# The fullest expert's remainder moved into its own wide job: 192 slots in one pass over the weights

## The chip, the cores and the metric

One core of one Trainium2 chip. The time is device microseconds for one execution of the whole kernel; lower is better.

## The reference, cut to what matters

Two decoder layers run on a prompt group (256 tokens) and a sample group (64 tokens), 320 tokens in all. Layer 0 has a dense channel mixer. Layer 1 has a mixture of eight experts, of which each token takes two. Only that mixture is touched:

```python
D_MODEL, N_EXPERTS, TOP_K, D_FF_EXPERT = 1024, 8, 2, 2816

def _moe(h, w_router, b_router, w_gate, w_up, w_down):
    logits = h @ w_router + b_router
    top_vals, top_idx = lax.top_k(logits, TOP_K)
    wts = jax.nn.softmax(top_vals, axis=-1)
    combine = sum(one_hot(top_idx, N_EXPERTS) * wts[..., None], axis=-2)
    out = 0
    for e in range(N_EXPERTS):
        out += combine[..., e:e + 1] * ((silu(h @ w_gate[e]) * (h @ w_up[e])) @ w_down[e])
    return out
```

All data are float32. One expert's three matrices are 3 x 1024 x 2816 x 4 bytes, 34.6 MB. The 640 assignments of the reference's inputs (the default seed) fall on experts 0 to 7 as 54, 170, 119, 49, 73, 62, 63 and 50.

## The kernel before, in words

Everything ahead of the experts (both mixers, the dense mixer, the router) is the same in both kernels and ends at about 1208 us of the span. After it the kernel runs **jobs**. A job takes one expert's weights from HBM once and puts a block of that expert's tokens through them.

- A **narrow** job has 64 slots. Its products are plain float32. The 64 gathered rows, transposed, are the stationary operand (XEF); the raw weights in MRAW move. The gate product goes to the lower 64 columns of the array and the up product to the upper 64, so one PSUM bank holds both. The profile shows each such float32 product as two passes.
- A **wide** job has 128 slots. Its products are float32r, in three passes: ScalarE rounds the weights to MHI (line 1775), VectorE writes the remainder to MLO over MRAW (line 1163), and TensorE multiplies high tokens by high weights (2637), low tokens by high weights (2638) and high tokens by low weights (2643).

Each job has 35 **pairs**, the unit of every semaphore count: 24 for gate and up (three groups of columns, widths 512, 512 and 384 per tile, eight contraction steps each) and 11 for down. A pair is 1 MB of weights (0.75 MB in the third group) in one slot of MRAW, which has 7 slots (`RAW_RING`). The SP queue issues two DMAs for a pair as soon as `m_used` says that TensorE has finished with the slot's last tenant, so loads run at most 7 pairs ahead.

Between pairs, TensorE does **side units**, each in PSUM bank 4 or 5: in pairs 2 to 9 it places the last job's result among all tokens ("combine", two products of 320 columns), in six pairs it transposes the product of gate and up ("turn"), and it builds the placement of this job's rows ("place") and the list of the next job's rows ("pick"). GpSimd gathers those rows by an indirect DMA (line 1991), and pairs 28 and 30 transpose them ("fill"). At the end of a job ScalarE scales the result to YEH (1816 wide, 1843 narrow) and VectorE writes its remainder YEL (1403 wide, 1420 narrow) and raises `y_made`; the next job can write the result's banks only then.

The order is written out: narrow 0, wide 1, then narrow and wide in a loop up to wide 5, then narrow 6, and a loop of further narrow jobs whose number comes from the router. Expert 0 takes job 0; the others are ranked by their number of tokens, the first three take jobs 1, 3 and 5, the rest jobs 2, 4, 6 and the first of the loop. An expert with more tokens than its job's slots gets extra narrow jobs of 64, which load its weights again. With the counts above, expert 1 (170 tokens, 128 slots) gets one: nine jobs, 0 to 8.

GpSimd's queue of gathers has a fixed length, `NE + EXTRA + 1`: those that no job asked for are let go together behind the last job by `V.tensor_copy(SPARE...).then_inc(idx_made, EXTRA)` (line 1448), and run one behind another.

Of the kernel before, what the change touches and what calls it, by code (L numbers as in the profile page):

```python
# [50 lines left out]
EXTRA = 7  # L51
# [10 lines left out]
def side_units():  # L62


    units = {p: [] for p in range(PAIRS)}
    for d in range(KD):
        units[d + 2].append(("combine", d))
    for t, p in enumerate((10, 11, 18, 19, 26, 27)):
        units[p].append(("turn", t))
    units[13].append(("place", 0))  # L70
    units[16].append(("pick", 0))
    plan, number = {}, 0
# [6 lines left out]
SIDE, JAUX = side_units()  # L79
assert JAUX % 2 == 0  # L80
FILLS = {28: 0, 30: 1}
HM_TILES = (2, 0, 1)
# [4 lines left out]
FILL_BANKS = (6, 7)  # L87
GT_BANKS = ((2, 3), (5, 1))
# [11 lines left out]
TURNED = {tile_at(k)[0]: s for units in SIDE.values() for s, what, k in units if what == "turn"}  # L100
TURN_SLOT = {k: s for units in SIDE.values() for s, what, k in units if what == "turn"}
# [138 lines left out]
def build(nc, a, out):  # L240
    ctx = ExitStack()
    with ctx:
# [152 lines left out]
        IOTAH = at("iotah", [P, P], F32, o + 13536)  # L395
# [37 lines left out]
        m_tile, xe_in, xe_out, y_hi = sem("m_tile"), sem("xe_in"), sem("xe_out"), sem("y_hi")  # L433
        xe_hi, idx_made, xg_in, hd_stored = sem("xe_hi"), sem("idx_made"), sem("xg_in"), sem("hd_stored")
# [36 lines left out]
        def _(sp):  # L471
# [49 lines left out]
            def load_job(job, e, first=False):  # L521
# [3 lines left out]
                for n in range(PAIRS):  # L525
                    if not (first and n < RAW_RING):
                        sp.wait_ge(m_used, job * PAIRS + (n - RAW_RING + 1))
                    for j in range(2):
                        if n < GPAIRS:
# [18 lines left out]
            with sp.Fori(1, MAIN) as job:  # L548
                e = sp.value_load(XI[0:1, bass.ds(job, 1)], min_val=0, max_val=NE - 1)
                load_job(job, e)  # L550
# [14 lines left out]
        def _(dve):  # L565
# [606 lines left out]

            def picked(src):
# [35 lines left out]
            V.tensor_copy(IOTAH[:, HALF:P], CF[:, C_IOTA:C_IOTA + HALF])  # L1209
            st(V.tensor_tensor(XG[:, 0:P], ident, CF[:, C_IOTA:C_IOTA + P], ALU.mult))  # L1210
# [46 lines left out]
            def ranks():  # L1257
# [9 lines left out]
                st(V.tensor_scalar(KEY[:, 3, :], KEY[:, 3, :], float(MAIN), 0.0, ALU.min, ALU.max))  # L1267
                st(V.memset(KEY[:, 2, 0:1], 1.0))
# [79 lines left out]
            def side_dve(job, p, split):  # L1348

                for s, what, k in SIDE[p]:  # L1350
                    bank = 4 + s % 2
                    if what == "combine":
                        dve.wait_ge(m_aux_in, job * JAUX + (s + 1))
                        V.tensor_tensor(SA[:, k, :], SA[:, k, :], PS[:, bank, 0:T], ALU.add).then_inc(m_aux_out, 1)  # L1354
                    elif what == "turn" and split is None:
                        f0, nf = tile_at(k)
                        dve.wait_ge(gate_out, job * TURNS + (k + 1))
                        V.tensor_tensor(GTF[:, f0:f0 + nf, :],  # L1358
                                        SGT[:, k % 2, 0:nf * HALF].rearrange("p (k n) -> p k n", k=nf),
                                        PS[:, bank, 0:nf * P].rearrange("p (k n) -> p k n", k=nf)[:, :, HALF:P],  # L1360
                                        ALU.mult).then_inc(m_aux_out, 1)
                    elif what == "turn":
                        f0, nf = tile_at(k)
                        dve.wait_ge(gt_hi, split * TURNS + (k + 1))
                        V.tensor_tensor(GTL[:, f0:f0 + nf, :],
                                        PS[:, bank, 0:nf * P].rearrange("p (k n) -> p k n", k=nf),
                                        GTH[:, f0:f0 + nf, :].bitcast(F32), ALU.subtract).then_inc(m_aux_out, 1)
                    elif what == "place":
                        dve.wait_ge(m_aux_in, job * JAUX + (s + 1))
                        V.tensor_copy(PTS[:, :], PS[:, bank, 0:T]).then_inc(m_aux_out, 1)  # L1370
                    else:
                        dve.wait_ge(m_aux_in, job * JAUX + (s + 1))
                        V.tensor_copy(IW[:, :], PS[:, bank, 0:2]).then_inc(m_aux_out, 1)
                        dve.wait_ge(m_aux_out, job * JAUX + (AHEAD + s + 1))
                        V.tensor_copy(IDX[:, :], IW[:, 1:2]).then_inc(idx_made, 1)
# [8 lines left out]
            def wide_dve(job, split):  # L1384
# [3 lines left out]
                for p in range(PAIRS):  # L1388
# [22 lines left out]
                    side_dve(job, p, split)  # L1411
# [3 lines left out]
            def narrow_dve(job, split_next=None, first=False):  # L1415

                for p in range(PAIRS):
# [8 lines left out]
                    side_dve(job, p, None)  # L1426
                    if p == 14:
                        choose(job + 1, split_next is None)
                    if first and p in TABLE_PAIRS:
                        tables(TABLE_PAIRS[p])  # L1430
                if split_next is not None:
                    for n in range(2):
                        m_lo_part(split_next, n)

            narrow_dve(0, 0, first=True)
            wide_dve(1, 0)
            with dve.Fori(1, WIDE) as two:
                narrow_dve(two * 2, two)
                wide_dve(two * 2 + 1, two)
            narrow_dve(2 * WIDE)  # L1440
            dve.wait_ge(sem("routed"), 1)
            extra = dve.value_load(XI[0:1, 15:16], min_val=1, max_val=1 + EXTRA)
            with dve.Fori(0, 1 + EXTRA) as k:
                with dve.If(k < extra):
                    narrow_dve(k + MAIN)
# [24 lines left out]
        def _(act):  # L1470
# [306 lines left out]
            def gathered(k, number, half):  # L1777

                act.wait_ge(xe_in, number + 1)
                src = PS[:, FILL_BANKS[k], :].rearrange("p (k n) -> p k n", k=4)  # L1780
# [18 lines left out]
            for k in range(2):  # L1799
                gathered(k, k, True)  # L1800

            def wide_act(job):
# [3 lines left out]
                for p in range(PAIRS):  # L1806
# [13 lines left out]
                    for s, what, k in SIDE[p]:  # L1820
                        if what == "turn":
                            f0, nf = tile_at(k)
                            act.wait_ge(m_aux_in, job * JAUX + (s + 1))
                            A.activation(GTH[:, f0:f0 + nf, :],
                                         PS[:, 4 + s % 2, 0:nf * P].rearrange("p (k n) -> p k n", k=nf), ACT.Copy)\
                                .then_inc(gt_hi, 1)
# [3 lines left out]
            def narrow_act(job, half_next):  # L1830
                A.activation(SPARE[:, 0:1], ONES[:, 0:1], ACT.Silu)
                for p in range(PAIRS):
# [11 lines left out]
                    for s, what, k in SIDE[p]:  # L1844
                        if what == "turn":
                            nf = tile_at(k)[1]
                            act.wait_ge(m_aux_in, job * JAUX + (s + 1))
                            if k >= 2:
                                act.wait_ge(m_aux_out, job * JAUX + (AHEAD + TURN_SLOT[k - 2] + 1))
                            A.activation(SGT[:, k % 2, 0:nf * HALF].rearrange("p (k n) -> p k n", k=nf),  # L1850
# [919 lines left out]
```

## Time and profile before

| | |
|---|---|
| time, median of three runs | 2053.22 us (2049.69 to 2054.38) |
| the profiled execution's own time | 2054.07 us |
| its span in the trace | 2052.2 us |
| TensorE busy | 1911.1 us, 93% of the span |
| VectorE, ScalarE busy | 969.0 us, 743.1 us |
| mean granted TensorE clock | 0.978 |
| read from HBM | 510.87 MB |

The busy share of TensorE is high in every stage, whether it works or not: ends of matrix products are modelled, and a run of passes counts as one busy stretch. What limits a stage is seen better from its DMA rate and from the distance between the starts of like instructions. The nine jobs take the stretch from 1208 to 2016 us. In a windows view the columns behind the stretch and its length are the busy time (and number) of TensorE's products, TensorE's weight loads, VectorE, ScalarE and GpSimd, then the granted clock as a share of full speed, the DMA share and GB/s.

### The profile page before, as it was taken

The numbers are of one execution on the slowest core, as the hardware profiler recorded it, in microseconds if no ns is written. First come the engines' busy times: TensorE is split into PE (matmuls) and PEld (weight loads), VectorE is DVE, ScalarE is ACT, GpSimd is POOL, SyncE is SP. The second block draws the span as 40 slices with busy tenths as digits, with TensorE's granted clock in tenths as the row PEclk, the third lists the DMA queues.
The fourth block names the chain that finished last, engine by engine and source line by source line (L and its number), as shares of the span: only waits on it lengthen the run. The fifth ranks groups of instructions, "written<-read, shape, count | busy, mean of one in ns | idle before, by whom it ended". The sixth has DMA issues, their size and how long they took to land. (4 is left out here: it accounts for less than half of the span.)

```text
span 2052.2 us, 31765 instructions
## 1 busy us (share of the span) xinstructions
PE 1911.1 (93%) x12573; PEld 1481.2 (72%) x12573; DVE 969.0 (47%) x1350; ACT 743.1 (36%) x928; POOL 132.3 (6%) x173
## 2 busy tenths in 40 slices
PE   7999999999999989999999999999899989989884
PEld 4999999997999979999999853684387358523221
DVE  4476554555444355765455432881385168401011
ACT  4434333434434353433344321661364156210011
POOL 3100002200000030000041100000000000000001
PEclk9999999999999999999999989999999999999997
DMA  9635355573666545334656369999989998999994
GB/s 353 208 99 170 116 182 181 177 250 99 210 204 213 172 131 184 103 108 154 185 190 212 139 231 407 358 355 406 409 307 394 408 391 325 408 407 407 409 408 170
DMA packets 243670, 525.43 MB, mean 256 GB/s; under 512 B 18103, under 2 KB 142121, under 8 KB 243538
## 3 DMA queue, kind: packets, MB, share of 16 engines
q1 hardware_dynamic: 233440, 492.63, 66.8%
q0 software_dynamic: 10080, 30.86, 4.7%
q8 instruction: 100, 1.64, 0.3%
q14 instruction: 32, 0.26, 0.0%
q10 hardware_dynamic: 18, 0.04, 0.0%
HBM read 510.87 MB, written 12.59 MB: 255 GB/s over the span
## 5 line engine op out<-in xcount | busy, mean ns | idle before, releaser
L577 DVE TENSOR_TENSOR wlo<-raw,whi 128x1024 fp32r<-128x1024 f32 x244 | 289.1, 1212 | 313.7 <-ACT whi L1484 312.4
L2094 PE MATMUL ps<-h1h,whi 128*128 128x320 f32 x1248 | 387.1, 322 | 6.8 <-DVE h1l L684 3.9
L2095 PE MATMUL ps<-h1l,whi 128*128 128x320 f32 x1248 | 372.3, 310 | 0.0
L1484 ACT ACTIVATE whi<-raw 128x1024 fp32r<-128x1024 f32 x244 | 247.7, 1046 | 118.6 <-PE ps L2479 44.8
L2683 PE MATMUL ps<-mraw,xef 128*64 128x512 f32 (+1 forms) x1152 | 251.9, 567 | 22.1 <-DMA mraw<-in_w_exp_up 16.7
L2094 PEld LDWEIGHTS ps<-h1h,whi 128*128 128x128 f32 x1248 | 236.6, 190 | 23.2 <-issue 17.5
L2095 PEld LDWEIGHTS ps<-h1l,whi 128*128 128x128 f32 x1248 | 236.7, 190 | 0.2 <-issue 0.2
L1163 DVE TENSOR_TENSOR mlo<-mraw,mhi 128x2048 fp32r<-128x2048 f32 (+1 forms) x105 | 225.4, 2165 | 16.4 <-ACT mhi L1775 16.4
L1775 ACT ACTIVATE mhi<-mraw 128x2048 fp32r<-128x2048 f32 (+1 forms) x105 | 190.6, 1819 | 84.8 <-DMA mraw<-in_w_exp_up 32.6
L2140 PE MATMUL ps<-h1h,wlo 128*128 128x320 f32 x1248 | 209.7, 310 | 0.0
L2140 PEld LDWEIGHTS ps<-h1h,wlo 128*128 128x128 f32 x1248 | 189.6, 188 | 0.4 <-issue 0.4
L2683 PEld LDWEIGHTS ps<-mraw,xef 128*64 128x64 f32 x1152 | 72.5, 136 | 146.2 <-issue 99.1
L2701 PE MATMUL ps<-mraw,gtf 128*64 128x512 f32 x528 | 127.8, 605 | 30.7 <-DMA mraw<-in_w_exp_down 28.7
L2637 PE MATMUL ps<-mhi,xeh 128*128 128x512 f32 (+1 forms) x288 | 115.3, 400 | 8.0 <-ACT mhi L1775 8.0
L2701 PEld LDWEIGHTS ps<-mraw,gtf 128*64 128x64 f32 x528 | 32.1, 136 | 109.7 <-DMA mraw<-in_w_exp_down 65.8
L2638 PE MATMUL ps<-mhi,xel 128*128 128x512 f32 (+1 forms) x288 | 110.4, 383 | 0.0
L1354 DVE TENSOR_TENSOR sa<-sa,ps 128x320 f32<-128x320 f32 x72 | 35.0, 486 | 119.5 <-PE ps L2554 119.5
L1358 DVE TENSOR_TENSOR gtf<-sgt,ps 128x256 f32<-128x256 f32 (+1 forms) x36 | 14.4, 399 | 160.4 <-ACT sgt L1850 160.4
L1840 ACT ACTIVATE sg<-ps 128x512 f32<-128x512 f32 (+1 forms) x36 | 20.2, 562 | 183.0 <-PE ps L2683 183.0
L2643 PE MATMUL ps<-mlo,xeh 128*128 128x512 f32 (+1 forms) x288 | 78.4, 384 | 1.6 <-DVE mlo L1163 1.6
L2094 PE MATMUL ps<-h2h,whi 128*128 128x320 f32 x256 | 77.0, 315 | 0.0
L2095 PE MATMUL ps<-h2l,whi 128*128 128x320 f32 x256 | 75.5, 309 | 0.0
(446 smaller groups left out, 2763.4 us busy)
## 6 DMA issues: line engine op xcount, KB each, us to landing
mraw<-in_w_exp_down SPq DMA_DIRECT2D x198, 512.0 KB, 12.7
mraw<-in_w_exp_gate SPq DMA_DIRECT2D x144, 512.0 KB, 7.4
mraw<-in_w_exp_up SPq DMA_DIRECT2D x144, 512.0 KB, 9.1
raw<-in_w_in SPq DMA_DIRECT2D x128, 512.0 KB, 3.9
raw<-in_w_ada SPq DMA_DIRECT2D x64, 512.0 KB, 3.8
mraw<-in_w_exp_gate SPq DMA_DIRECT2D x72, 384.0 KB, 7.2
mraw<-in_w_exp_up SPq DMA_DIRECT2D x72, 384.0 KB, 9.2
pause<-in_w_ada SPq DMA_DIRECT2D x32, 512.0 KB, 7.0
```

The lines of the kernel that those rows point to most:

```text
L577: V.tensor_tensor(WLO[:, u % RAW_UNITS, 0:w], RAW[:, u % RAW_UNITS, 0:w], WHI[:, h % HI_UNITS, 0:w].bitcast(F32), ALU.subtract).then_inc(l ...
L1163: V.tensor_tensor(MLO[:, n % RAW_RING, 0:w], MRAW[:, n % RAW_RING, 0:w], MHI[:, n % HI_RING, 0:w].bitcast(F32), ALU.subtract).then_inc(m_l ...
L1484: A.activation(WHI[:, h % HI_UNITS, 0:w], RAW[:, u % RAW_UNITS, 0:w], ACT.Copy).then_inc(hi_made, 1)
L1775: A.activation(MHI[:, n % HI_RING, 0:w], MRAW[:, n % RAW_RING, 0:w], ACT.Copy).then_inc(m_hi, 1)
L2094: M.matmul(out_, w, v[0], start=start, stop=False, skip_group_check=True)
L2095: M.matmul(out_, w, v[1], start=False, stop=False, skip_group_check=True)
L2140: ins = M.matmul(PS[:, 2 * j + m, 0:T], w[1][:, s], parts[0][:, k * T:(k + 1) * T], start=False, stop=(k == KD - 1), skip_group_check=True)
L2637: M.matmul(o_, XEH[:, k, :], hi_[:, s], start=(k == 0), stop=False)
L2638: M.matmul(o_, XEL[:, k, :], hi_[:, s], start=False, stop=False)
L2643: ins = M.matmul(PS[:, GROUP_BANKS[g][2 * i + j], 0:w], XEH[:, k, :], lo_[:, s], start=False, stop=(k == KD - 1))
L2683: ins = M.matmul(PS[HALF * j:HALF * j + HALF, GROUP_BANKS[g][2 * i], 0:w], XEF[:, k, :], MRAW[:, p % RAW_RING, s], start=(k == 0), stop=(k ...
L2701: ins = M.matmul(PS[HALF * h:HALF * h + HALF, DOWN_BANKS[0], :], GTF[:, kf, :], MRAW[:, p % RAW_RING, s], start=(kf == 0), stop=(kf == KF ...
```

## The change

The fullest of experts 1 to 7 keeps job 1, which now has 192 slots and is called **both**. The first 128 are done in three passes as before; slots 128 to 191 are done in plain float32 from the same raw weights in MRAW. The table of extra jobs gives this expert one block fewer, and `EXTRA` goes from 7 to 6. Jobs 3 and 5 stay wide.

- MRAW must now stay raw, so the remainder goes to two of the five MHI slots: three slots for the high part (`BOTH_HI`), two for the remainder (`BOTH_LO`).
- A pair of gate and up in job 1 is two contraction steps of one tile instead of one step of two tiles; the loads have the same number and bytes, with runs of 512 (384) columns instead of 1024 (768).
- The order on TensorE within a pair: raw pass, high passes, remainder pass.
- Job 0 has no combine (nothing precedes it), but a second pick (pair 12), gather (XG2) and fill (pairs 20 and 21) for slots 128 to 191. Job 1 has six more turns and one more place. Job 2's combine has four products instead of two.
- ScalarE and VectorE make a third result part (YEH2, YEL2) at the end of job 1, and job 1's first product waits for job 0's `y_made`.
- Jobs 2 and 3 are written out; the loop runs once, for jobs 4 and 5.

```diff
-EXTRA = 7
+EXTRA = 6
+BOTH_BANKS = ((3, 7, 2), (0, 1, 6))
+BOTH_HI, BOTH_LO = 3, 2
...
+                        if both and n < GPAIRS:
+                            (c0, w), k = cols_at(n // 4), 2 * (n % 4)
+                            sp.dma_start(MRAW[:, n % RAW_RING, 2 * w * j:2 * w * (j + 1)].rearrange("p (k n) -> p k n", k=2),
+                                         (g, u)[j][:, k:k + 2, c0:c0 + w]).then_inc(m_raw[n % RAW_RING], 16)
...
+            def both_lo_part(job, n):
+                w = 4 * GROUPS[n // KD][1] if n < GPAIRS else 2 * D
+                dve.wait_ge(m_hi, n + 1)
+                if n >= BOTH_LO:
+                    dve.wait_ge(m_used, job * PAIRS + (n - BOTH_LO + 1))
+                V.tensor_tensor(MHI[:, BOTH_HI + n % BOTH_LO, 0:w], MRAW[:, n % RAW_RING, 0:w],
+                                MHI[:, n % BOTH_HI, 0:w].bitcast(F32), ALU.subtract).then_inc(m_lo, 1)
...
+                st(V.tensor_scalar(KEY[:, 5, :], KEY[:, 1, :], 1.5, None, ALU.is_lt))
+                st(V.tensor_tensor(KEY[:, 2, :], KEY[:, 2, :], KEY[:, 5, :], ALU.subtract))
...
+            def both_hi_part(job, n):
+                if n >= BOTH_HI:
+                    act.wait_ge(m_used, job * PAIRS + (n - BOTH_HI + 1))
...
+                        A.activation(SG2[:, 0:w], PS[:, BOTH_BANKS[t % 2][2], 0:w], ACT.Copy).then_inc(copied2, 1)
...
-            for job in range(NE + EXTRA + 1):
+                if job == 1:
+                    pool.wait_ge(idx_made, 2)
+                    pool.indirect_dma_start(XG2[:, :], None, HD, bass.IndirectOffsetOnAxis(IDX2[:, 0:1], 0)).then_inc(xg_in, 16)
+                    pool.wait_ge(xg_in, 32)
...
+                def gate_up_both(p):
+                    t, (_, w) = p // 4, cols_at(p // 4)
+                    gate_, up_, both_ = BOTH_BANKS[t % 2]
+                    raw_, hi_, lo_ = raw_in(p)
+                    if p == 0:
+                        pe.wait_ge(y_made, job + 1)
+                    for n in range(2):
+                        k = 2 * (p % 4) + n
+                        for j in range(2):
+                            M.matmul(PS[HALF * j:HALF * j + HALF, both_, 0:w], XEF2[:, k, :],
+                                     raw_[:, (2 * j + n) * w:(2 * j + n + 1) * w], start=(k == 0), stop=(k == KD - 1),
+                                     skip_group_check=True)
+                    pe.wait_ge(m_hi, p + 1)
+                    for n in range(2):
+                        k = 2 * (p % 4) + n
+                        for j, bank in enumerate((gate_, up_)):
+                            s = slice((2 * j + n) * w, (2 * j + n + 1) * w)
+                            M.matmul(PS[:, bank, 0:w], XEH[:, k, :], hi_[:, s], start=(k == 0), stop=False)
+                            M.matmul(PS[:, bank, 0:w], XEL[:, k, :], hi_[:, s], start=False, stop=False)
+                    pe.wait_ge(m_lo, p + 1)
...
-            narrow_pe(0, False)
-            wide_pe(1, 0, True)
-            with pe.Fori(1, WIDE) as two:
-                narrow_pe(two * 2, False)
-                wide_pe(two * 2 + 1, two, True)
+            narrow_pe(0, SIDE_FIRST, None)
+            both_pe(1)
+            narrow_pe(2, SIDE, "both")
+            wide_pe(3, 1, "narrow")
+            with pe.Fori(2, WIDE) as two:
```

## Rows read from the trace of the kernel before

**Rows 1.** The page, DMA issues: times issued, KB each, us to landing.
```profile
mraw<-in_w_exp_down SPq DMA_DIRECT2D x198, 512.0 KB, 12.7
```

**Rows 2.** Stretches of one expert job each: busy of each engine, clock, DMA, GB/s.
```profile
1286.00:1393.00 107.00, 104.51 (x479) 85.23 (x481) 85.97 (x64) 69.50 (x52) 0.94 (x1) 0.97 0.95 359
1393.00:1471.00 78.00, 70.98 (x333) 23.71 (x329) 10.71 (x26) 7.72 (x18) 0.95 (x1) 1.00 1.03 407
...
1844.00:1930.00 86.00, 73.33 (x339) 23.56 (x335) 8.65 (x24) 7.30 (x17) 0.95 (x1) 1.00 1.03 408
1930.00:2016.00 86.00, 72.81 (x335) 23.37 (x331) 8.69 (x24) 7.03 (x15) 0.95 (x1) 1.00 0.97 386
```

**Rows 3.** TensorE's timeline at the ends of jobs 0, 1 and 2: start, us, idle before.
```profile
1283.65 1.03 PE L2701 MATMUL ps<-mraw,gtf 128*64 128x512 f32 x4
1287.41 0.47 PE L2637 MATMUL ps<-mhi,xeh 128*128 128x512 f32 x1 [2.74 <-ACT mhi L1775]
...
1289.65 1.22 PE L2643 MATMUL ps<-mlo,xeh 128*128 128x512 f32 x2 [1.07 <-DVE mlo L1163]
...
1392.23 1.94 PE L2683 MATMUL ps<-mraw,xef 128*64 128x512 f32 x8
...
1468.70 1.94 PE L2701 MATMUL ps<-mraw,gtf 128*64 128x512 f32 x8 [0.62 <-DMA mraw<-in_w_exp_down]
```

**Rows 4.** VectorE's timeline: the last operation of jobs 0, 1, 7 and 8.
```profile
1285.51 0.75 DVE L1420 SCALAR_TENSOR_TENSOR yel<-ps,sw,yeh 128x512 fp32r<-128x512 f32 x1 [9.12 <-ACT yeh L1843]
...
1393.06 1.41 DVE L1403 SCALAR_TENSOR_TENSOR yel<-ps,sw,yeh 128x512 fp32r<-128x512 f32 x2 [6.39 <-ACT yeh L1816]
...
1929.72 0.75 DVE L1420 SCALAR_TENSOR_TENSOR yel<-ps,sw,yeh 128x512 fp32r<-128x512 f32 x1 [17.52 <-ACT yeh L1843]
...
2015.71 0.75 DVE L1420 SCALAR_TENSOR_TENSOR yel<-ps,sw,yeh 128x512 fp32r<-128x512 f32 x1 [17.44 <-ACT yeh L1843]
```

**Rows 5.** ScalarE's timeline at the end of wide job 1.
```profile
1392.34 1.27 ACT L1816 ACTIVATE yeh<-ps,sw 128x512 fp32r<-128x512 f32 x2 [7.86 <-PE ps L2668]
```

**Rows 6.** TensorE's timeline in narrow job 2 (xcount: passes in the run).
```profile
1394.52 3.65 PE L2683 MATMUL ps<-mraw,xef 128*64 128x512 f32 x16 [0.36 <-DVE yel L1403]
1398.11 0.42 PE L2553 MATMUL ps<-pts,yeh 128*128 128x320 f32 x1
...
1398.60 1.94 PE L2683 MATMUL ps<-mraw,xef 128*64 128x512 f32 x8
1400.46 0.41 PE L2553 MATMUL ps<-pts,yeh 128*128 128x320 f32 x1
...
1433.03 1.51 PE L2683 MATMUL ps<-mraw,xef 128*64 128x384 f32 x8
```

**Rows 7.** TensorE's timeline in wide job 1: two turns; a pair's start, the next side unit.
```profile
1327.31 0.60 PE L2586 MATMUL ps<-cf,sg 128*128 128x128 f32 x4
...
1330.50 0.60 PE L2586 MATMUL ps<-cf,sg 128*128 128x128 f32 x4
...
1333.70 0.39 PE L2637 MATMUL ps<-mhi,xeh 128*128 128x512 f32 x1
...
1336.43 0.49 PE L2589 MATMUL ps<-cf,pm 128*128 128x128 f32 x3
```

**Rows 8.** Two stretches at the start of wide job 1 (columns as in Rows 2).
```profile
1285.00:1290.00 5.00, 1.51 (x5) 1.03 (x6) 3.26 (x3) 4.18 (x3) 0.00 (x0) 0.86 1.03 411
1290.00:1296.00 6.00, 6.00 (x16) 4.62 (x16) 5.16 (x3) 4.00 (x3) 0.00 (x0) 0.55 1.02 405
```

**Rows 9.** Groups of instructions by line: busy, mean ns, idle before.
```profile
L1163 DVE TENSOR_TENSOR mlo<-mraw,mhi 128x2048 fp32r<-128x2048 f32 x81 | 183.9, 2287 | 12.9 <-ACT mhi L1775 12.9
...
L1775 ACT ACTIVATE mhi<-mraw 128x2048 fp32r<-128x2048 f32 x81 | 155.0, 1917 | 60.2 <-DMA mraw<-in_w_exp_up 24.7 <-DMA mraw<-in_w_exp_down 24.1 <-PE ps L2643 10.7
```

**Rows 10.** GpSimd's timeline after the last job.
```profile
2020.29 0.95 POOL L1991 DMA_INDIRECT xg<-h_rows,idx  x1 [46.72 <-DVE spare L1448]
...
2044.91 0.95 POOL L1991 DMA_INDIRECT xg<-h_rows,idx  x1 [3.29 <-DMA xg<-h_rows,idx]
```

More of the change, by code:

```diff
@@ L59, with side_units @@
 AHEAD = 2
-def side_units():
+def side_units(turns, others, start=0):
     units = {p: [] for p in range(PAIRS)}
-    for d in range(KD):
-        units[d + 2].append(("combine", d))
-    for t, p in enumerate((10, 11, 18, 19, 26, 27)):
+    for p, what, k in others:
+        units[p].append((what, k))
+    for t, p in enumerate(turns):
         units[p].append(("turn", t))
-    units[13].append(("place", 0))
-    units[16].append(("pick", 0))
-    plan, number = {}, 0
+    plan, number = {}, start
     for p in range(PAIRS):
@@ L1346, in table_out @@
                 see.next(sem("routed"))
[L1348 to L1375, printed above, removed]
@@ L1410, in wide_dve @@
                         next_weight(job)
-                    side_dve(job, p, split)
+                    for s, what, k in SIDE[p]:
+                        if what == "combine":
+                            combine_dve(job * JAUX, s, k)
+                        elif what == "turn":
+                            low_turn(s, k, gt_hi, split * TURNS + (k + 1))
+                        elif what == "place":
+                            place_dve(PTS, job * JAUX, s)
+                        else:
+                            pick_dve(IW, IDX, idx_made, job * JAUX, s)
@@ L1417, in narrow_dve @@
+            def narrow_dve(job, side, split_next=None):
                 for p in range(PAIRS):
@@ L1425, in narrow_dve @@
                         low_fill(FILLS[p - 1], split_next)
-                    side_dve(job, p, None)
+                    for s, what, k in side[p]:
+                        if what == "combine":
+                            combine_dve(job * JAUX, s, k)
+                        elif what == "turn":
+                            half_turn(GTF, s, k, gate_out, job * TURNS + (k + 1))
+                        elif what == "place":
+                            place_dve(PTS, job * JAUX, s)
+                        elif what == "pick2":
+                            pick_dve(IW2, IDX2, idx_made, job * JAUX, s)
+                        else:
+                            pick_dve(IW, IDX, idx_made, job * JAUX, s)
+                    if side is SIDE_FIRST and p in TABLE_PAIRS:
+                        tables(TABLE_PAIRS[p])
+                    if side is SIDE_FIRST and p == 9:
+                        choose2(job + 1)
                     if p == 14:
                         choose(job + 1, split_next is None)
[L1429 to L1436, printed above, removed]
+            narrow_dve(0, SIDE_FIRST, 0)
+            for n in range(BOTH_LO):
+                both_lo_part(1, n)
+            both_dve(1)
             with dve.Fori(1, WIDE) as two:
-                narrow_dve(two * 2, two)
+                narrow_dve(two * 2, SIDE, two)
+                for n in range(2):
+                    m_lo_part(two, n)
                 wide_dve(two * 2 + 1, two)
-            narrow_dve(2 * WIDE)
+            narrow_dve(2 * WIDE, SIDE)
             dve.wait_ge(sem("routed"), 1)
@@ L2573, in _, with turn, place, side_pe @@
             pe.wait_ge(sem("gt_out"), 4)
-            def side_pe(job, p, half_before):
-                for s, what, k in SIDE[p]:
+            def turn(bank, src, nf):
+                for m in range(nf):
+                    ins = M.transpose(PS[:, bank, m * P:(m + 1) * P], src[:, m * P:(m + 1) * P], ident)
+                return ins
+            def place(bank, marks):
+                for t in range(TT):
+                    ins = M.transpose(PS[:, bank, t * P:(t + 1) * P], marks[:, t, :].bitcast(F32), ident)
+                return ins
+            def side_pe(job, p, before, side=SIDE):
+                for s, what, k in side[p]:
                     bank = 4 + s % 2
@@ L2581, in side_pe @@
                         pe.wait_ge(y_made, job + 1)
-                        ins = combine(k, bank, half_before)
+                        ins = combine_both(k, bank) if before == "both" else combine(k, bank, before == "narrow")
                     elif what == "turn":
                         pe.wait_ge(prod_made, job * TURNS + (k + 1))
-                        for m in range(tile_at(k)[1]):
-                            ins = M.transpose(PS[:, bank, m * P:(m + 1) * P], SG[:, k % 2, m * P:(m + 1) * P], ident)
+                        ins = turn(bank, SG[:, k % 2, :], tile_at(k)[1])
@@ L2587, in side_pe @@
                     elif what == "place":
-                        for t in range(TT):
-                            ins = M.transpose(PS[:, bank, t * P:(t + 1) * P], PM[:, t, :].bitcast(F32), ident)
-                    else:
-                        pe.wait_ge(p_made, job + 2)
+                        ins = place(bank, PM)
+                    elif what == "pick2":
+                        pe.wait_ge(p_made, 2)
+                        ins = pick(PS[:, bank, 0:2], PM2)
+                    else:
+                        pe.wait_ge(p_made, job + 3)
+                        ins = pick(PS[:, bank, 0:2])
@@ L2675, in narrow_pe @@
+            def narrow_pe(job, side, before):
                 pe.wait_ge(xe_out, job * 2 + 2)
@@ L2697, in narrow_pe @@
                                 pe.wait_ge(prod_made, job * TURNS + 4)
-                            turned_in(job, kf)
+                            turned_in(job * JAUX, kf, slots_of(side, "turn"))
                             for h in range(2):
```

320 lines of the change are left out of this document (266 added, 54 removed).

## The prediction, written before the result was known

> **What bounds the kernel now.** I read the DMA issues first: 198 loads of down matrices at 22 a job are nine jobs for eight experts [rows 1]. The reference's counts say whose the ninth is: expert 1 has 170 tokens and 128 slots, and no other expert exceeds its block (119 and 73 in 128; 63, 62, 54, 50, 49 in 64).
>
> Then the windows, job by job [rows 2]. Narrow jobs 7 and 8 take 86 us each, with DMA share near 1 and 386 to 408 GB/s: they are bound by the loads, 86.0 / 35 = 2.457 us a pair. The reader should not take TensorE's 73 us there for a limit. Wide job 1 takes 107 us at 359 GB/s, DMA below full: it is bound by TensorE. Narrow job 2 takes only 78 us because some pairs were loaded during job 1. The last look is at the tail: after job 8 GpSimd runs six gathers nobody asked for, the first issued at 2020.29 and the last at 2044.91, 4.9 us apart on average [rows 10], and nothing issues behind them.
>
> **What is removed.** Job 8 as a whole: from job 7's last operation to job 8's, 2015.71 - 1929.72 = **86.0 us** [rows 4]. All of it is on the path, since its loads are what the core waits for; its 70 DMAs on the SP queue, ScalarE's and VectorE's work and one gather go with it and were hidden beneath them.
>
> **What is added to job 1.** Its own work today: TensorE ends job 0 at 1283.65 + 1.03 = 1284.68, begins job 1 at 1287.41 and begins job 2 at 1392.23 [rows 3]. That is 104.8 us. In it are 1.1 us of waiting for the first remainder [rows 3] and about 2.9 us lost to the lower clock (6 us at a granted 0.55 lose 2.7, the second half of the stretch before about 0.2 [rows 8]). At full clock and without waits job 1 is 100.8 us of TensorE.
>
> 1. Raw passes. A narrow pair of width 512 is eight passes. A run of 16 takes 3.65 us and one of 8 takes 1.94 [rows 6], so a pair costs 1.71 and the rest is the last pass's tail. Width 384: 1.51 - 0.23 = 1.28. So 27 x 1.71 + 8 x 1.28 = **56.4 us**.
> 2. Changes of array shape. Raw products run as 128*64, the others as 128*128, so a pair has two changes more. The trace has no raw pass beside a high pass; the nearest row is the combine in a narrow job. From one combine to the next 2.35 us pass (1398.11 to 1400.46) [rows 6], 1.71 of them raw, so 0.64 is left for two products of 320 columns and two changes. A wide pair of 12 products of 512 columns takes 2.73 us (1333.70 to 1336.43) [rows 7], 0.2275 each; two of 320 columns are 0.28 by that, and 0.36 are the changes. I take 0.36 x 35 = **12.6 us**. The bounds are 0 (a change that hides behind the stream) and 0.64 (all of it): 0 to 22.4.
> 3. Six more turns: a pair with a turn takes 3.19 (1327.31 to 1330.50), without 2.73 [rows 7]: 0.46 x 6 = **2.8 us**. One more place is three transposes, at most a turn: **0.3**.
> 4. The start. The new job's first product waits for job 0's `y_made`, raised at 1285.51 + 0.75 = 1286.26 [rows 4]; it needn't wait for ScalarE's copy, so it starts at 1286.3 instead of 1287.4. While the raw pass runs (1.7) ScalarE makes the first high part (1.92) and VectorE the remainder (2.29) behind it [rows 9], done near 1290, about when TensorE has done raw and high passes.
>
> The sum is 1286.3 + 100.8 + 56.4 + 12.6 + 2.8 + 0.3 = 1459.2, against 1392.23: **+67.0 us**.
>
> Of TensorE's clock: after 2.74 us of idle and a few scattered products it was granted 0.86, then 0.55 [rows 3, 8], so partly the lower level, 1.2 GHz. The idle is now 1.6 us and the work behind it dense, so I charge nothing and keep 4 us for the upper end.
>
> **What stays hidden in job 1.** A pair takes 1.71 + 2.73 + 0.36 = 4.8 us on TensorE. VectorE's remainder for pair n may start when TensorE begins pair n-1, and is wanted 1.71 + 0.2 + 1.8 = 3.7 us into pair n: 8.5 us for 2.29 of work. Ahead of it in VectorE's order is at most the wait for ScalarE's silu at a tile's end, the product of gate and up, and a turn, whose high part stands behind another 1.92 us copy: together near 4 us. ScalarE's high part has two pairs' time. A load has seven pairs of 4.8 us for 2.46 us of transfer, so the shorter runs (2 KB and 1.5 KB) cost nothing; only pair 0 could land later, beneath the wait for `y_made`. SP issues as many DMAs as before. The second pick, gather and fill go into job 0, which waits for loads anyway (TensorE 1.71 of 2.46 us a pair), and it loses eight combines. The two new table operations and the second selection on VectorE are there too. GpSimd's extra gather stands ahead of job 2's, eight pairs earlier.
>
> **Job 2.** Its start finds the ring full instead of partly full, but `y_made` comes later. Now ScalarE takes 1.27 us for two parts [rows 5], and VectorE ends at 1393.06 + 1.41 = 1394.47 [rows 4], 2.24 after TensorE. With a third part on each, 3.5. The first slots come free when two more pairs' halves are done, at 3.5 + 1.8 = 5.3 us. From there 28 pairs must be loaded: 68.8 us, plus some 2 to 4 us until a transfer lands in an empty queue, plus 1.94: 78 to 80. Before it was 1468.70 + 1.94 - 1392.23 = 78.4 [rows 3]. So **0**, within 2 us. The four-product combine makes TensorE's pair about 2.8 instead of 2.35; the two slots freed at once cover most of eight times 0.3.
>
> **The tail.** Released gathers before: fixed length 16, less ten used. After: 15 plus the separate one, less ten used (first, second selection, eight jobs). Six again, so the last job's end to the span's end stays 36 us.
>
> Sum: -86.0 + 67.0 + 0 = **-19.0 us**. On the profiled execution, 2054.07, that is 2035.1; it lay 0.85 above the median of 2053.22, so **2034 us**.
>
> On item 2 the Trainium skill has a rule against this change: TensorEngine Tiling (Array Packing), under Key Properties, says that changing the tiling mode, as opposed to the tile, drains TensorE; and TensorE: Matmul & The Clock Gate, under Single matmul latency, puts the drain near 175 ns. An estimate from these pages is 70 changes x 0.175 = 12.3 us, with which the time would be 0.3 us lower. The trace agrees with a cost at each change (0.36 for two), and no run here shows yet that high passes behind raw ones pay the same.
>
> **The rivals.**
> - *Forecast* (0.70): job 1 dense on TensorE, as summed. Alone it spans 2024 to 2045.
> - *Dear changes and a lower clock* (0.12): 0.64 a pair instead of 0.36 gives +9.8, the clock +4: 2048. For it: each change comes with a semaphore wait. Against: wide jobs wait twice a pair without a gap.
> - *Late copies in the smaller ring* (0.06): only three high and two remainder slots. If both copies ran after the preceding pair had ended, the remainder would be ready 1.92 + 2.29 = 4.2 us into the pair instead of 3.7 wanted: 0.5 x 35 = +18, 2052, no change. Against: the waits permit an earlier start.
> - *The two halves of the array don't overlap* (0.04), the slower side. If a raw pass between two changes of shape ran its gate and up products one after the other, it would take twice as long: +56.4, 2090. It decides from a third of the passes on (19 / 56.4). Against: raw runs between two combines are also eight passes long and show the full rate [rows 6].
> - *Nine jobs stay* (0.01): then 86.0 is not taken off: 2120. Against: 170 is at most 192.
> - *More is given back* (0.07): changes almost free and job 2 gains 2 us: 2023 to 2026.
>
> The range is 2022 to 2048: it leaves out the slower cases and half of the dear one, near 0.17. Faster by over 0.2% (4 us, about what a measurement of this kernel can tell from no change) is forecast, dear and giving back: 0.89. Same 0.06, slower 0.05.
>
> **What the profile after would show.** 176 loads of down matrices. Job 1 from `y_made` to the next raw run near 173 us, with clock near 1.00 and DMA near 200 GB/s (34.6 MB in 173 us). Pairs of width 512 without side units start 4.8 us apart: 5.1 means dear changes, 6.5 halves in turn. TensorE's waits for the high part or remainder in job 1 near zero. Job 2 near 78 us, job 7 (now the last) 86, six gathers and 36 us behind it. The prediction is wrong if the pair's spacing is off by over 0.4 us, or if TensorE waits at each tile's end.

## The result, and the profile after

The changed kernel takes **2034.55 us** (median of five runs, 2029.12 to 2037.92) against 2053.22 (2049.69 to 2058.04): a ratio of 0.9901, 95% interval 0.9878 to 0.9925. The forecast was 2034, range 2022 to 2048.

The page's DMA issues show eight jobs, 176 / 22 [rows 1], and 476.26 MB read from HBM instead of 510.87:

```profile
HBM read 476.26 MB, written 12.59 MB: 241 GB/s over the span
...
mraw<-in_w_exp_down SPq DMA_DIRECT2D x176, 512.0 KB, 12.0
```

The windows after, job 1 (both), job 2, and the last job, 7 (columns as in [rows 2]):

```profile
1283.00:1456.00 173.00, 172.40 (x784) 102.67 (x786) 90.29 (x71) 73.87 (x63) 0.94 (x1) 1.00 0.68 230
1456.00:1537.00 81.00, 74.64 (x351) 26.36 (x347) 11.37 (x27) 8.25 (x19) 0.95 (x1) 1.00 0.98 378
...
1906.00:1992.00 86.00, 73.29 (x335) 23.67 (x335) 8.76 (x23) 7.35 (x17) 0.94 (x1) 1.00 0.98 388
```

Job 1 is where the work went: TensorE full, clock 1.00, and DMA only 0.68 busy, where the two stretches it replaces had DMA near full [rows 2]. Its 230 GB/s are more than the 200 that the forecast gave as a sign: 39.8 MB in 173 us instead of 34.6. In the first 17 us of the job DMA still runs at about 386 GB/s, so the ring was not yet full when job 1 began. VectorE's timeline gives the last operation of jobs 0, 1, 2 and 7, as in [rows 4]:

```profile
1282.71 0.75 DVE L1524 SCALAR_TENSOR_TENSOR yel<-ps,sw,yeh 128x512 fp32r<-128x512 f32 x1 [9.16 <-ACT yeh L2007]
...
1456.83 1.41 DVE L1495 SCALAR_TENSOR_TENSOR yel<-ps,sw,yeh 128x512 fp32r<-128x512 f32 x2 [8.64 <-ACT yeh L1981]
1458.15 0.74 DVE L1497 SCALAR_TENSOR_TENSOR yel<-ps,iw,yeh 128x512 fp32r<-128x512 f32 x1
...
1537.69 0.75 DVE L1524 SCALAR_TENSOR_TENSOR yel<-ps,sw,yeh 128x512 fp32r<-128x512 f32 x1 [9.12 <-ACT yeh L2007]
...
1992.59 0.75 DVE L1524 SCALAR_TENSOR_TENSOR yel<-ps,sw,yeh 128x512 fp32r<-128x512 f32 x1 [17.42 <-ACT yeh L2007]
```

With the same operations of every job the difference of the two profiled spans, 2028.9 - 2052.2 = -23.3 us, divides without a remainder. Lengths in us, from one job's last operation to the next one's:

| | to end of job 0 | 1 | 2 | 3 | 4 | 5 | 6 | 7 | 8 | behind the last job |
|---|---|---|---|---|---|---|---|---|---|---|
| before | 1285.51 | 107.55 | 78.41 | 106.76 | 80.87 | 106.81 | 77.78 | 86.03 | 85.99 | 36.49 |
| after | 1282.71 | 174.12 | 80.86 | 106.28 | 78.10 | 106.28 | 78.37 | 85.87 | none | 36.31 |
| difference | -2.80 | +66.57 | +2.45 | -0.48 | -2.77 | -0.53 | +0.59 | -0.16 | -85.99 | -0.18 |

Jobs 1, 2 and 8 are where the forecast put the change. Their sum is -17.0, and the medians moved by 18.7. The first column is the scatter of single executions: in the traces of the changed kernel and its variants below, job 0 ends anywhere from 1281.11 to 1291.33. That scatter is why the lengths of jobs are compared below, and whole times only where they differ by more.

Job 4's -2.77 is another matter. Job 4 takes 80.87 and 79.82 us in the two traces of the old loop (before, and experiment 10) and 77.5 to 79.3 in all ten of the new one. Before, TensorE stood idle ahead of job 4's first product, and no releaser is shown for it; in the changed kernel the first eight passes start at once:

```profile
1579.66 5.37 PE L2683 MATMUL ps<-mraw,xef 128*64 128x512 f32 x24 [2.18 <-issue]
```

```profile
1643.14 1.94 PE L2980 MATMUL ps<-mraw,xef 128*64 128x512 f32 x8
1645.43 3.65 PE L2980 MATMUL ps<-mraw,xef 128*64 128x512 f32 x16 [0.35 <-DVE yel L1464]
```

Experiment 10, with the old loop, has 2.30 us of idle there, and none of the ten others has more than 0.36. It is the place where the old loop over two jobs begins its second round; the new one has a single round, since jobs 2 and 3 are written out. So some 2 us of the gain probably come from writing them out. No run isolates this.

TensorE's timeline of job 1's first pairs, after:

```profile
1279.94 1.94 PE L2998 MATMUL ps<-mraw,gtf 128*64 128x512 f32 x8 [0.67 <-DMA mraw<-in_w_exp_down]
1283.60 1.94 PE L2918 MATMUL ps<-mraw,xef 128*64 128x512 f32 x8 [1.72 <-DVE yel L1524]
1285.47 0.50 PE L2926 MATMUL ps<-mhi,xeh 128*128 128x512 f32 x1
...
1287.42 1.07 PE L2933 MATMUL ps<-mhi,xeh 128*128 128x512 f32 x4
1288.41 1.94 PE L2918 MATMUL ps<-mraw,xef 128*64 128x512 f32 x8
...
1293.27 1.94 PE L2918 MATMUL ps<-mraw,xef 128*64 128x512 f32 x8
```

The reader sees the 1.72 us for `y_made` at the start, the raw run of eight passes at its old length of 1.94, so both halves of the array still work together, and no bracket of idle time in any line behind it. Pairs of 512 columns without a side unit are 4.81 to 4.86 us apart. In the whole job the view of waits lists none of TensorE's products waiting for a copy (weight loads do, by 0.8 us at most, beneath the products); what it lists first, behind GpSimd's wait for the next list of rows, are the copies waiting for TensorE:

```profile
ACT mhi L1900 <- PE ps L2933: 42.3, 16, 3.5
DVE mhi L1223 <- PE ps L2933: 32.1, 17, 2.6
```

### The profile page after: what moved, and what is told of

It is laid out like the page before. It is cut to its first block and busy times, and to the rows that moved or that the text cites. A ratio compares the mean times of both kernels' runs of the same rounds, so it can differ in the third digit from the quotient of the medians.

```text
span 2028.9 us, 31221 instructions
## 1 busy us (share of the span) xinstructions
PE 1902.8 (94%) x12557; PEld 1474.9 (73%) x12557; DVE 962.2 (47%) x1336; ACT 741.4 (37%) x927; POOL 131.8 (6%) x173
## 3 DMA queue, kind: packets, MB, share of 16 engines
HBM read 476.26 MB, written 12.59 MB: 241 GB/s over the span
## 5 line engine op out<-in xcount | busy, mean ns | idle before, releaser
L2980 PE MATMUL ps<-mraw,xef 128*64 128x512 f32 (+1 forms) x960 | 208.2, 566 | 15.6 <-DMA mraw<-in_w_exp_up 11.9
L1199 DVE TENSOR_TENSOR mlo<-mraw,mhi 128x2048 fp32r<-128x2048 f32 (+1 forms) x70 | 150.2, 2165 | 10.1 <-ACT mhi L1892 10.0
L2980 PEld LDWEIGHTS ps<-mraw,xef 128*64 128x64 f32 x960 | 62.3, 136 | 118.3 <-issue 84.1
L2998 PE MATMUL ps<-mraw,gtf 128*64 128x512 f32 x440 | 106.6, 605 | 25.1 <-DMA mraw<-in_w_exp_down 23.6
L1223 DVE TENSOR_TENSOR mhi<-mraw,mhi 128x2048 fp32r<-128x2048 f32 (+1 forms) x35 | 75.9, 2168 | 56.8 <-PE ps L2933 32.1
L2998 PEld LDWEIGHTS ps<-mraw,gtf 128*64 128x64 f32 x440 | 26.7, 136 | 91.0 <-DMA mraw<-in_w_exp_down 58.1
L2862 PE MATMUL ps<-mhi,xeh 128*128 128x512 f32 (+1 forms) x192 | 75.5, 393 | 5.5 <-ACT mhi L1892 5.5
L2863 PE MATMUL ps<-mhi,xel 128*128 128x512 f32 (+1 forms) x192 | 72.6, 378 | 0.0
L2004 ACT ACTIVATE sg<-ps 128x512 f32<-128x512 f32 (+1 forms) x30 | 16.8, 562 | 143.3 <-PE ps L2980 143.3
```

Of the source, the lines that this page charges most:

```text
L1199: V.tensor_tensor(MLO[:, n % RAW_RING, 0:w], MRAW[:, n % RAW_RING, 0:w], MHI[:, n % HI_RING, 0:w].bitcast(F32), ALU.subtract).then_inc(m_l ...
L1223: V.tensor_tensor(MHI[:, BOTH_HI + n % BOTH_LO, 0:w], MRAW[:, n % RAW_RING, 0:w], MHI[:, n % BOTH_HI, 0:w].bitcast(F32), ALU.subtract).the ...
L2862: M.matmul(o_, XEH[:, k, :], hi_[:, s], start=(k == 0), stop=False)
L2863: M.matmul(o_, XEL[:, k, :], hi_[:, s], start=False, stop=False)
L2980: ins = M.matmul(PS[HALF * j:HALF * j + HALF, GROUP_BANKS[g][2 * i], 0:w], XEF[:, k, :], MRAW[:, p % RAW_RING, s], start=(k == 0), stop=(k ...
L2998: ins = M.matmul(PS[HALF * h:HALF * h + HALF, DOWN_BANKS[0], :], GTF[:, kf, :], MRAW[:, p % RAW_RING, s], start=(kf == 0), stop=(kf == KF ...
```

## The experiments

Each of the first eight is one edit of the changed kernel, 9 is three of them together, and 10 is an edit of the kernel before. Experiments 1, 2, 5, 6 and 7 were executed once each (1968.93, 2058.16, 2037.35, 2029.26 and 2038.62 us), so they are read by the lengths in their traces alone. In the traces of experiments 2, 3, 4, 5 and 8 and of the changed kernel, where job 2 is the same, it takes 80.8 to 81.5 us from one job's last operation to the next: differences of a few tenths say nothing.

**1. Job 1 without the raw passes.** The products into the third bank are left out in all 35 pairs, so the outputs lack slots 128 to 191.

```diff
-                            M.matmul(PS[HALF * j:HALF * j + HALF, both_, 0:w], XEF2[:, k, :], raw_[...], ...)
...
-                            ins = M.matmul(PS[HALF * h:HALF * h + HALF, BOTH_BANKS[0][2], :], GTF2[:, kf, :], raw_[...], ...)
```

> Job 1 without its raw passes (slots 128 to 191 are not computed; 42 tokens lack one expert's part). It measures terms 1 and 2 of the sum together. My theory (raw stream 56.4 us plus 70 changes of array shape): TensorE's job 1, 171.8 us in the changed kernel, falls by 68 to 70 us to 102 to 104, and TensorE waits for nothing new in it. Rival, the smaller ring of copies: with pairs now 2.73 us apart instead of 4.86 the three high and two remainder slots become the limit, TensorE waits for the high part or the remainder in many pairs, and the job falls by less, to 110 or more.

```profile
1286.88 0.47 PE L2920 MATMUL ps<-mhi,xeh 128*128 128x512 f32 x1 [2.80 <-ACT mhi L1900]
...
1391.92 1.94 PE L2970 MATMUL ps<-mraw,xef 128*64 128x512 f32 x8
```

TensorE's job 1 runs from 1286.88 to 1391.92, 105.0 us, against 171.8 (1283.60 to 1455.42). Without raw passes the start must wait for ScalarE's copy again, 2.80 us, and the clock falls again:

```profile
1285.00:1290.00 5.00, 3.12 (x9) 2.52 (x10) 3.46 (x3) 3.65 (x2) 0.00 (x0) 0.76 1.05 387
1290.00:1296.00 6.00, 6.00 (x26) 4.93 (x25) 5.23 (x4) 4.17 (x4) 0.00 (x0) 0.92 1.06 388
```

The granted 0.76 and 0.92 take 5 x 0.24 + 6 x 0.08 = 1.7 us, so at full clock the job has 103.3, and the raw passes with their changes of shape cost 68.5. The forecast's two terms were 56.4 + 12.6 = 69.0. As measured the job fell by 66.8, less than the 68 to 70 expected: the expectation did not have the lower clock. Behind the start no product waits for a copy in the job, so the smaller ring is no limit even at 2.73 us a pair.

**2. One slot for each copy.**

```diff
-BOTH_HI, BOTH_LO = 3, 2
+BOTH_HI, BOTH_LO = 1, 1
```

> One high slot and one remainder slot instead of three and two, so that both copies of a pair can only begin when TensorE has ended the pair before. Theory: the remainder is then ready 1.92 + 2.29 = 4.2 us or a little more into the pair and wanted at about 3.75, so TensorE waits some 0.5 us in each ordinary pair and about 1.5 us more in the six pairs behind a tile's end, where silu and the third copy stand ahead on ScalarE: job 1 gets 18 to 30 us longer (190 to 202). Rival, copies that hide anyway: less than 5 us longer. Rival, copies already at the limit in the changed kernel: much more than 30 us, since then the slack I count isn't there.

```profile
1303.11 0.50 PE L2926 MATMUL ps<-mhi,xeh 128*128 128x512 f32 x1 [0.19 <-ACT mhi L1900]
...
1305.43 1.20 PE L2933 MATMUL ps<-mhi,xeh 128*128 128x512 f32 x4 [0.21 <-DVE mhi L1223]
```

Both kinds of wait, absent in the changed kernel, are there, 28 times and 9.6 us in all; the rest of the longer job is not listed as a wait of TensorE's products. Job 1's length is 193.56 instead of 174.12: +19.4, at the low end of what was expected. So the ring matters, and rings of three and two are enough. The rival of late copies fell because the slots removed its cause, not because the copies are fast.

**3. The table as before.** The fullest expert gets its extra job although job 1 does all its slots, so 42 tokens count expert 1 twice.

```diff
-                st(V.tensor_tensor(KEY[:, 2, :], KEY[:, 2, :], KEY[:, 5, :], ALU.subtract))
```

> Only the table is as before: the fullest expert is given its extra job again, although job 1 does all its 192 slots (the result of 42 tokens counts expert 1 twice). It measures the removed term. Theory: one more load-bound job of 86.0 us behind the others and five gathers instead of six behind it: 2034.5 + 86 - 0 to 4 = 2116 to 2121, some 3.1 to 3.3% above the kernel before. Rival, that the removed job was partly hidden: less than 80 us is added.

Measured 2114.58 us (2113.82 to 2118.05), ratio 1.031 (1.0288 to 1.0331). In its trace the last operations of jobs 7 and 8 stand at 1994.90 and 2080.89: 85.99 us, the length that was taken off. The whole time rose by 80.0 only, since what follows the last job is 31.8 us long (2112.7 - 2080.89) instead of 36.3. The tail has one gather fewer:

```profile
2085.64 0.95 POOL L2159 DMA_INDIRECT xg<-h_rows,idx  x1 [46.87 <-DVE spare L1564]
...
2105.52 0.95 POOL L2159 DMA_INDIRECT xg<-h_rows,idx  x1 [3.46 <-DMA xg<-h_rows,idx]
```

That is 86.0 - 4.5 = 81.5 by the traces and 80.0 by the medians. The time lies 1.4 us under the 2116 to 2121 expected, which had taken off 4 us at most for the tail. By the median alone 80.0 is just at the rival's "less than 80", but the job's own length in the trace decides: the removed job was not hidden at all, and the tail is what adds up differently.

**4. Alternating order.** Even pairs raw, high, remainder; odd pairs high, remainder, raw.

```diff
+                    if p % 2 == 0:
+                        raw_pass()
                     pe.wait_ge(m_hi, p + 1)
...
-                    return ins
+                    return ins if p % 2 == 0 else raw_pass()
```

> Order of passes alternates: even pairs raw, high, remainder; odd pairs high, remainder, raw. Nothing else changes; the number of changes of array shape in job 1 falls from 80 to 61 (counted from the order of passes and side units). Theory, 0.2 us a change: job 1 is 3 to 5 us shorter on TensorE, 167 to 169 instead of 171.8, and pairs meet without the 0.15 to 0.2 us step where raw follows raw. Rival, the cost isn't the change of shape but each start of a pair (its waits): no change, 171.5 to 172. In the whole time 4 us is at the edge of what shows.

```profile
1288.37 1.94 PE L2919 MATMUL ps<-mraw,xef 128*64 128x512 f32 x8 [1.73 <-DVE yel L1524]
...
1294.93 1.07 PE L2938 MATMUL ps<-mhi,xeh 128*128 128x512 f32 x4
1295.93 3.65 PE L2919 MATMUL ps<-mraw,xef 128*64 128x512 f32 x16
1299.51 0.50 PE L2931 MATMUL ps<-mhi,xeh 128*128 128x512 f32 x1
```

Two raw passes meet as one run of 16 at 3.65 us, as they do inside a narrow job [rows 6]. Job 1 on TensorE runs from 1288.37 to 1456.12: 167.75, **-4.07** us. Counted in the traces, the changes between 128*64 and 128*128 fell from 64 to 45, and 16 others, to and from the combine's 64*128, stayed: 0.21 us for each of the 19. Experiment 9, with the same order, has job 1 shorter by 4.0. The waits of a pair are as many as ever, so the rival (each pair's start costs) falls. The whole time was 2031.64 us (2027.84 to 2035.82); alone it can't be told from 2034.55.

**5. A late start.** Job 1's first product also waits for the first remainder.

```diff
                     if p == 0:
                         pe.wait_ge(y_made, job + 1)
+                        pe.wait_ge(m_lo, 1)
```

> Job 1's first raw pass also waits for the first remainder, so TensorE stands idle some 5 us instead of 1.72 at the job's start; from then on it is as dense as before. Theory: the clock is granted lower behind so long a gap (in the leave-out run 2.80 us of idle was enough) and the first pairs run at twice the spacing for a few us: job 1 ends 3.3 us later by the wait and 1.5 to 4 us more by the clock, and pairs run at the higher level after that. Rival, dense work alone keeps the clock: only the 3.3 us of the wait, with the granted clock at 1.00 throughout.

```profile
1286.91 3.68 PE L2919 MATMUL ps<-mraw,xef 128*64 128x512 f32 x8 [5.13 <-DVE mhi L1223]
...
1293.52 1.94 PE L2919 MATMUL ps<-mraw,xef 128*64 128x512 f32 x8
```

```profile
1285.00:1290.00 5.00, 3.09 (x8) 0.86 (x8) 4.05 (x2) 3.92 (x3) 0.00 (x0) 0.50 1.05 386
1290.00:1295.00 5.00, 5.00 (x22) 2.72 (x20) 1.30 (x1) 1.31 (x1) 0.00 (x0) 0.93 1.05 387
```

The same raw run takes 3.68 us instead of 1.94 at a granted 0.50, that is 1.2 GHz, and the next one 1.94 again. Job 1 is 179.32 instead of 174.12 long: 5.2, of which 3.4 are the longer wait and 1.8 the clock. The rival, that dense work alone keeps the clock, falls. Against the forecast's reserve of 4 us for the clock, this fall cost 1.8.

**6. The third part first.** At the end of job 1 YEH2 and YEL2 come first, with a semaphore of their own, for which job 2's first product into that bank waits.

```diff
-                    pe.wait_ge(y_made, job + 1)
+                elif before == "both":
+                    pe.wait_ge(sem("y2_made"), 1)
```

> At the end of job 1 the third result part is made first on both engines, with a semaphore of its own, and job 2's first product into its bank waits for that alone. Theory of job 2's extra 3.0 us (81.4 against 78.4): the first loads can only be issued when pairs 0 and 1 are done, so an earlier start counts in full. TensorE's idle at the start falls from 1.59 us to 0 and job 2 gets 1.5 us shorter (80). Rival, the combine sets the pace: job 2 unchanged, 81.4.

```profile
1455.52 1.08 PE L2966 MATMUL ps<-mhi,gth 128*128 128x512 f32 x4
1456.53 5.37 PE L2985 MATMUL ps<-mraw,xef 128*64 128x512 f32 x24
```

Job 2 starts with 24 passes and no gap, where the changed kernel has this:

```profile
1455.42 1.94 PE L2980 MATMUL ps<-mraw,xef 128*64 128x512 f32 x8
1458.95 3.65 PE L2980 MATMUL ps<-mraw,xef 128*64 128x512 f32 x16 [1.59 <-DVE yel L1497]
1462.53 0.41 PE L2721 MATMUL ps<-pts,yeh 128*128 128x320 f32 x1
...
1463.51 1.94 PE L2980 MATMUL ps<-mraw,xef 128*64 128x512 f32 x8
1465.38 0.42 PE L2721 MATMUL ps<-pts,yeh 128*128 128x320 f32 x1
```

From TensorE's change-over to job 2's last operation it takes 1536.67 - 1456.53 = 80.1 us instead of 1537.69 - 1455.42 = 82.3: -2.1. That is a little more than the 1.6 of the gap, by less than the scatter of job 2. Experiment 9, with the same edit, has job 2 shorter by 2.2.

**7. Two products in job 2's combine.** The result of slots 128 to 191 is not added.

```diff
-                M.matmul(o_, YEL[:, s], PTS[:, :], start=False, stop=False)
-                M.matmul(o_, YEH2[rows_, s2], PTS2[rows_, :], start=False, stop=False)
-                return M.matmul(o_, YEL2[rows_, s2], PTS2[rows_, :], start=False, stop=True)
+                return M.matmul(o_, YEL[:, s], PTS[:, :], start=False, stop=True)
```

> Job 2's combine has two products again (the result of slots 128 to 191 is not added to the tokens). It measures what the other two cost. Theory: TensorE's pairs 2 to 9 then start 2.35 us apart instead of 2.85, under the 2.46 of the loads, and job 2 gets 1 to 2 us shorter (79.5 to 80.5), as the part of job 2's 3.0 us that isn't the late start. Rival, the loads hide the combine: job 2 unchanged, 81.4.

Combines start 2.36 us apart instead of 2.85, and the same stretch of job 2 takes 1544.35 - 1464.05 = 80.3 us: -2.0. So job 2's extra 3.0 us have two causes of about equal size. Together they are more than 3.0 (2.1 + 2.0); whether they overlap or it is scatter wasn't tried.

**8. Only the gathers that are asked for.** Each gather behind the eighth stands under a condition on the router's number of extra jobs, and line 1565's release is gone.

```diff
-            for job in range(NE + EXTRA + 1):
+            for job in range(MAIN + 1):
...
+            for k in range(1 + EXTRA):
+                with pool.If(k < extra):
+                    pool.wait_ge(idx_made, k + MAIN + 3)
+                    pool.indirect_dma_start(XG[:, :], None, HD, ...).then_inc(xg_in, 16)
+                    pool.wait_ge(xg_in, 16 * (k + MAIN + 3))
...
-            V.tensor_copy(SPARE[:, 0:1], SW[:, :]).then_inc(idx_made, EXTRA)
```

> GpSimd's gathers: eight in a row as before, then one for each extra job that the router asked for, each under a condition; the gathers that nobody asked for are gone. Theory, from the run with nine jobs, whose tail had five of them instead of six and was 4.5 us shorter: the tail is set by these gathers down to the last output's store, which lands at 2014.2 of 2028.9, so the kernel gets 12 to 15 us shorter, about 2021. Rival, something else ends with them (the stores or the end of the program): less than 5 us.

The changed kernel's tail, GpSimd's timeline, first and last of six, and the SP queue's last store:

```profile
1998.07 0.94 POOL L2160 DMA_INDIRECT xg<-h_rows,idx  x1 [48.01 <-DVE spare L1565]
...
2022.09 0.94 POOL L2160 DMA_INDIRECT xg<-h_rows,idx  x1 [3.38 <-DMA xg<-h_rows,idx]
```

```profile
2009.34 0.54 SPq L596 DMA_DIRECT2D out_ys<-xtm  x1
```

And with the edit, where GpSimd's last gather stands at 1954.44, in job 7, and the last store is the last thing issued:

```profile
2012.99 0.53 SPq L596 DMA_DIRECT2D out_ys<-xtm  x1
```

Measured **2015.93 us** (2013.46 to 2018.13), ratio 0.9822 (0.9805 to 0.9839). Behind the last job are 2016.3 - 1997.95 = 18.4 us instead of 36.3: -18.0, more than the 12 to 15 expected. Not all of it is the gathers. The store is issued 15.0 us behind the last job's last operation instead of 16.8. TensorE's timeline says why; the same run of 24 products in the changed kernel, here, and in experiment 9, which has this edit too:

```profile
1994.82 4.50 PE L3024 MATMUL ps<-cf,sa 128*128 128x128 f32 x24 [3.06 <-issue]
...
2000.13 2.83 PE L3027 MATMUL ps<-cf,sa 128*128 128x128 f32 x24 [3.01 <-issue]
...
1989.88 4.50 PE L3044 MATMUL ps<-cf,sa 128*128 128x128 f32 x24 [3.06 <-issue]
```

The granted clock over these three stretches was 0.62, 1.00 and 0.61. In experiment 9 the gathers are gone as well, and the store is 16.8 us behind again. So 1.7 of the 18.0 us is the clock that this one execution was granted, and 16.3 are the gathers'.

**9. All three edits**, and **10. the tail's edit in the kernel before.**

> The changed kernel with three edits together: alternating order of passes, third result part first, no gathers that nobody asked for. Theory, that they lie at three places of one path and add up: -4.1 (job 1), -2.1 (job 2), -18 (tail), so 2034.6 - 24.2 = 2010, a ratio near 0.979 to the kernel before. Rival, part of the gain is given back to the loads of later jobs: 2014 or more.

> The kernel before with the tail's edit alone. Theory: the tail is independent of the change, so it gives the same 18 us here, 2053.2 - 18 = 2035, ratio 0.991, which is also what the whole change gave; the change is then worth 2035 - 2016 = 19 us with the shorter tail as well. Rival, the gathers matter less behind nine jobs: 2040 or more.

| | median us | range | ratio to before |
|---|---|---|---|
| changed kernel | 2034.55 | 2029.12 to 2037.92 | 0.9901 (0.9878 to 0.9925) |
| 9, three edits | 2009.93 | 2006.32 to 2017.94 | 0.9811 (0.9788 to 0.9834) |
| 10, before with the tail's edit | 2034.81 | 2030.47 to 2038.54 | 0.9921 (0.9900 to 0.9942) |

Each ratio is to executions of the kernel before taken beside it (medians 2053.22 and, for 9 and 10, 2051.99). Both came out as expected, 9 closer than its trace bears out: 24.6 us by the medians, 21.2 by the spans. In that trace job 1 is 170.14 (-4.0), job 2 78.66 (-2.2) and the tail 20.1 (-16.3), together -22.5; job 0 has 1.6 less. Jobs 3 and 4 have 107.8 and 79.3, 2.7 more than in the changed kernel and a little more than in any other of its variants (107.65 and 78.75 at most), so in this execution a part may have been given back, as the rival had it; the median stays under its 2014. The tail's edit in the old kernel gives as much as the whole change did. With the short tail on both sides the change is worth 2034.81 - 2015.93 = 18.9 us, as without it (18.7), so nothing of the one is part of the other.

## Why the prediction was right

The mechanism came out as forecast: a job bound by loads went away, and its 42 tokens cost TensorE time in a job bound by TensorE. That 2034 and 2034.55 agree within 0.6 us is partly luck. The three terms of the forecast add up to -17.0 and not to -19.0, and some 2 us that the forecast didn't have, at the start of job 4, make up for it.

- **The removed job, 86.0.** Right and shown by 3: 85.99 come back when the table asks for it.
- **Raw passes, 56.4, and changes of shape, 12.6.** Together 69.0 forecast, 68.5 measured by 1. Split otherwise than forecast: side-free pairs are 4.86 us apart, so the two changes cost 4.86 - 2.73 - 1.71 = 0.42 and not 0.36. But not every pair gains two: in the eight pairs with a combine TensorE changed shape around it before too. The count is 80 in job 1 now, of which 16 were there before, so 64 new ones and not 70. By experiment 4's 0.21 each that would be 13.7, and 70.1 with the raw passes; it is 1.6 us more than the 68.5 measured, and no run says why. The Trainium skill says (TensorEngine Tiling (Array Packing), Key Properties) that a change of tiling mode drains TensorE, and (TensorE: Matmul & The Clock Gate, Single matmul latency) that the drain is near 175 ns. Experiment 4 agrees that each change costs, and measured 0.21 us for it.
- **The start.** Forecast 1.6 us of idle, measured 1.72. The clock stayed at the full level, as taken: granted 1.00 through job 1. In experiments 1 and 5 it fell behind 2.80 and 5.13 us of idle at the same place.
- **Job 1 as a whole.** 1281.88 (1279.94 + 1.94) to 1455.42 is 173.5 us on TensorE against 107.5: +66.0, forecast +67.0. Its other terms, 100.8 + 2.8 + 0.3 = 103.9, stand against 103.3 in experiment 1.
- **Job 2, 0 within 2.** The one term outside its bounds: 1455.42 to 1536.86 is 81.4 against 78.4, +3.0. The step that failed is "the two slots freed at once cover most of eight times 0.3". It took the load as the only limit behind the first release. Experiments 6 and 7 show that both things it named and then set against each other count: the late `y_made` 2.1 and the four-product combine 2.0. The combine's pace of 2.85 was foreseen (2.8), its effect not.
- **Job 4, no term.** -2.77 in the two traces compared, some 2 us of it the idle at its start. The forecast took all jobs behind job 2 as unchanged.
- **The tail.** Six gathers before and after, 36.5 and 36.3 us: right. That the number of gathers sets most of this stretch is shown by 3 (one fewer, 4.5 us) and by 8 and 9 (none, 16.3 us).
- **The rivals.** Dear changes with a lower clock: not in this kernel (0.42 a pair, clock 1.00). Late copies: refuted as the kernel stands, and real at one slot each (2). Halves in turn: refuted by the raw run's 1.94 us in job 1. Nine jobs: refuted by the page. More given back: no.

## What to carry to other kernels

Where one stage waits for loads and another for TensorE, reloading weights for a remainder costs the load's full length (86.0 us here), and putting the remainder through the weights while they are there costs its products (68.5): compare these two, stage by stage, and not the busy shares. At a hand-over, ask which single buffer the next stage needs first and give that one its own semaphore; a few us of late release come back as late loads. Before shortening the middle, look at what runs behind the last useful instruction: here the unused gathers of a queue of fixed length cost 16.3 us, nearly as much as the whole change gained. And when a kernel's loops are rewritten on the way, compare the jobs that should be the same too: job 4 got shorter here without being asked to.

## What the runs showed of the hardware that I had not expected

- A change between products of 128*64 and of 128*128 costs 0.21 us, and placing two runs of one shape side by side gets it back (experiment 4, on average over 19 changes).
- Indirect gathers of 128 rows that wait for one another are issued 4.8 us apart on average ((2022.09 - 1998.07) / 5), of which GpSimd works 0.94.
- After 1.72 us of idle TensorE's clock stayed at 2.4 GHz (job 1 of the changed kernel). It also did after 2.18 and 2.30 us, at the start of job 4 in the kernel before and in experiment 10. After 2.80 it fell to 1.2 a little way into the new work (experiment 1), and after 5.13 it was there from the first product (3.68 us for a run of 1.94, experiment 5).
- The length of the idle alone doesn't decide it. Behind the last job the same 24 products followed 3.01 us of idle at a granted 1.00 in experiment 8 (2.83 us), and 3.06 us at 0.61 in experiment 9 (4.50 us).
